# Two depthwise convolutions accumulated in PSUM by VectorE, without tap matmuls, in a three-block transformer kernel

## Chip, cores, metric

One core of one Trainium2 chip runs the whole program. The metric is the device time of one execution in microseconds (us), the median of several.

## The reference, cut to what matters

Three blocks follow one another on x (512 tokens, 1024 channels, float32). The change touches two causal depthwise convolutions: one of 31 taps over 512 channels in the first layer of block 1, and one of 4 taps over 2048 channels in block 3. It also touches the norm of the memory (256 tokens) that cross-attention reads.

```
def _mixer_hgrn2_conv(h, w_in, w_out, lb, out_norm, dw_w, dw_b, ln_g, ln_b):
    proj = h @ w_in
    qz, fz, iz, gz, glu_a, glu_b = split(proj)            # 512 columns each
    f = lb + (1.0 - lb) * sigmoid(fz)
    o = _hgrn2_chunkwise(silu(qz), f, iz)                 # ... gated by silu(gz)
    c = glu_a * sigmoid(glu_b)
    c = _causal_depthwise_conv(c, dw_w, dw_b)             # 31 taps: y_t = sum_k w_k x_{t-30+k} + b
    o_b = silu(_layernorm(c, ln_g, ln_b))
    return concatenate([o_a, o_b]) @ w_out
# mem_n = _rmsnorm(mem, mem_norm); k, v = split(mem_n @ wkv)
# third block: qk = silu(causal_depthwise_conv(concatenate([aq, ak]), conv_w))   # 4 taps
```

## The kernel before, in words

Activations stand as tiles of 128 channels by 512 tokens: `T(i)` is slot i of the SBUF tensor A. Every product with weights is cut into units of 1024x128 weights (`UNITS`). For each unit SP's queue loads RW, ScalarE rounds it to WH (`w_hi`, L261), GpSimd subtracts to get WL (L2709), and TensorE makes 24 matmuls: 8 tiles of input by three passes (L266, L267, L268). WH and WL have three slots, so the weights of unit u + 3 are rounded only after unit u is done. The results go to PSUM banks 0 to 3 in turn; `bank_free` makes unit e wait until VectorE or ScalarE has emptied the bank of unit e - 4. GpSimd does nothing but these subtractions.

The order of work is written by hand. `PLAN` is a list of stages; every engine walks it in order and runs its own part. `Steps.wait_ge` waits for a semaphore; `settle` waits for the engine's own last instruction. `Linear`, `Pairs` and `TokenMajor` are the product stages. With `late=`, the row norm is applied when a unit leaves PSUM (VectorE, L393 or L474), and an activation function follows on ScalarE. In `Linear`, ScalarE applies the function of unit j (which needs VectorE's copy of it) before it rounds the weights of unit j + 3. The hooks `between`, `between_act` and `between_pe` put further work of an engine behind each unit.

In layer 0 the order is: `l0.glu` (8 units, in four pairs, of the gating layer: VectorE scales two banks, ScalarE takes a sigmoid, VectorE multiplies into T(0) to T(3), L496), the memory norm `mem` (class `Late`: on ScalarE `hi` L858 and squares L860, on VectorE `lo` L866 and sums L876 over 8 tiles of 128x256), then `l0.q`, `l0.f`, the memory's `rstd`, `h_gates`, `l0.i`, `h_cum`, `h_query`, `l0.g`, `h_scaled`, `x0.k` (8 units of 256 columns from the memory) and the recurrence (`h_turn`, `h_pe`, `h_vec`).

The 31 taps of the convolution are shared. VectorE does 23 with `depthwise` (L1193, L1199), each tap on all four tiles, from T(k) into T(4 + k), both in SBUF; `conv(st, n)` issues n such rounds: three behind the memory norm and one behind each unit. TensorE does the last eight, as matmuls with diagonal matrices in full float32 (`tap_pe`, L1232), one tile behind each unit of `l0.q`; ScalarE writes those diagonals (`tap_diag`, L1223), and VectorE adds the sums (`tap_add`, L1239). The memory's `rstd` matmuls (L889, L893) wait for the last of these adds because they use banks 6 and 7.

In block 3, `conv3` does the 4 taps behind every second unit of `t.qk` (16 units) with the same `depthwise`, SBUF to SBUF, and `qk_silu` (L2345) follows on ScalarE. Then ScalarE works through `gif_act` (L2354 to L2365), VectorE through `gif_dve`, ScalarE through `stacked_hi`, and `t.v` (TokenMajor, L531 to L533) begins on TensorE as soon as its banks are free. ScalarE rounds the fourth unit of `t.v` behind `stacked_hi`.

Of the kernel before, what the change touches and what calls it, by code (L numbers as in the profile page):

```python
# [27 lines left out]
P = 128  # L28
# [139 lines left out]
def program(nc, io, names):  # L168
    ctx = ExitStack()
    with ctx:  # L170
# [250 lines left out]
        class Pairs:  # L421
# [3 lines left out]
            def __init__(self, name, n, dst, func, of=0, yh=None, acc=False, ready=None, u_off=0, func2=None, late=None, first=1):  # L425
# [8 lines left out]
            def tensor(self, pe, st):  # L434
# [6 lines left out]
                for j in range(first, 2 * self.n):  # L441
                    xh, xl = self.yh if (self.yh is not None and j % 2 == 0) else (XH, XL)
                    pe_tile(pe, st, self.u0 + j, self.e0 + j, xh, xl, S)

            def scalar(self, act, st):
# [5 lines left out]
                for i in range(self.n):  # L451
# [17 lines left out]
                    w_hi(act, st, u + 1 + SPLIT)  # L469

# [5 lines left out]
            def vector(self, dve, st):  # L476
# [4 lines left out]
                for i in range(self.n):  # L481
# [19 lines left out]
                    names[f"ev{e}"] = names[f"ev{e + 1}"]  # L501

# [336 lines left out]
        class Late:  # L839


            def __init__(self, id, gain, ready, left, sq, x, hi, lo, acc, r, rc, b, cols, after, lag):
# [3 lines left out]
                PLAN.append(self)  # L846
# [4 lines left out]
            def scalar(self, act, st):  # L851
                for k in range(KT):
                    if self.after is not None and k < KT - 1:
                        st.wait_ge(*reached(f"{self.after}.free{k}"))
                    if k == 4:
                        w_hi(act, st, self.unit)
                    st.wait_ge(*reached(self.ready(k)))
                    st.do(nc.scalar.activation(self.hi[:, k, 0:self.cols], self.x(k), ACT.Copy, scale=vec(self.gain, k)), f"{self.id}.hi{k}")  # L858
                    if k in self.left:
                        st.do(nc.scalar.activation(self.sq(k), self.x(k), ACT.Square), f"{self.id}.sq{k}")  # L860
# [54 lines left out]
        def late(id, gain, ready, left, sq, x=lambda k: X[:, k, :], hi=None, lo=None, acc=None, r=None, rc=None, b=4, cols=S, after=None,  # L915
                 lag=KT):
            return Late(id, gain, ready, left, sq, x, XH if hi is None else hi, XL if lo is None else lo,
                        SD[:] if acc is None else acc, NR[:, 0, :] if r is None else r, rc, b, cols, after, lag)
# [250 lines left out]
        def lb_ratio(st):  # L1169
# [13 lines left out]
        Pairs("l0.glu", 4, at(0), ACT.Sigmoid, of=1, ready="n0", late=n0)  # L1183
        mark("glu.done", "vector")
        memsq = A[:, 32:36, :].rearrange("p a (b c) -> p (a b) c", c=MEM)
        mem = late("mem", "mem_norm", ready=lambda k: "mem.in", x=lambda k: memt[:, k, :], hi=MH, lo=ML, left=range(KT),
                   sq=lambda i: memsq[:, i, :], acc=T(37)[:, 0:MEM], r=NR[:, 1, 0:MEM], rc=SM[:, 156:158], b=6, cols=MEM)

        def depthwise(st, src, dst, taps, w, b, n, k0=0, first=None, last=0):

            for k in range(n if first is None else 0):
                x, y = src(k), dst(k)
                st.do(v.tensor_scalar(y, x, vec(w, (k0 + k) * taps + taps - 1), vec(b, k) if b else 0.0, ALU.mult, ALU.add))  # L1193
            for t in range(taps - 2 if first is None else first, last - 1, -1):
# [7 lines left out]
        tap = [None]  # L1202

        def conv(st, n):

            for i in range(n):
                if tap[0] is None:
                    depthwise(st, lambda k: T(k), lambda k: T(4 + k), 31, "conv_dw_w", "conv_dw_b", 4, first=None, last=30)
                    tap[0] = 29
                elif tap[0] >= PT:  # L1210
                    depthwise(st, lambda k: T(k), lambda k: T(4 + k), 31, "conv_dw_w", "conv_dw_b", 4, first=tap[0], last=tap[0])
                    tap[0] = tap[0] - 1

        vs(lambda st: conv(st, 3))
        PT = 8

        def tap_diag(st, k):
            for n in range(PT):
                if k >= 2:
                    st.wait_ge(*reached(f"tap.sum{k - 2}"))  # L1220
                elif n == 0:
                    st.wait_ge(consts_in, 16)
                st.do(a_.activation(W2(24 + 2 * (k % 2), 2)[:, n * P:(n + 1) * P], ident, ACT.Copy, scale=vec("conv_dw_w", k * 31 + n)),  # L1223
                      f"tap.diag{k}")

        def tap_pe(st, k):
            if k == 0:
                st.wait_ge(*reached("n0.r"))
            st.wait("glu.done", f"tap.diag{k}")
            for n in range(PT - 1, -1, -1):  # L1230
                sh = 30 - n
                last = mm(PS[:, 4 + k, sh:S], W2(24 + 2 * (k % 2), 2)[:, n * P:(n + 1) * P], T(k)[:, :S - sh], start=(n == PT - 1), stop=(n == 0))  # L1232
            st.do(last, f"tap.sum{k}")

        def tap_add(st, k):
            st.wait_ge(*reached(f"tap.sum{k}"))
            st.settle()
            sh = 31 - PT
            st.do(v.tensor_tensor(T(4 + k)[:, sh:], T(4 + k)[:, sh:], PS[:, 4 + k, sh:S], ALU.add), f"tap.added{k}")  # L1239

        def first_diags(act, st, e):
            tap_diag(st, 0)
            w_hi(act, st, U0["l0.q"] + 1)
            tap_diag(st, 1)
        Stage(scalar=first_diags)

        def q_act(st, j):
            if j < 2:
                tap_diag(st, j + 2)
        Linear("l0.q", dst=at(8), func=ACT.Silu, late=n0, between=lambda st, j: conv(st, 1), between_act=q_act, between_pe=tap_pe)  # L1250
        def f_dve(st, j):
            tap_add(st, j)
            conv(st, 1)
        Linear("l0.f", dst=at(12), func=ACT.Sigmoid, late=n0, between=f_dve)

        def mem_pe(pe, st, e):
            st.wait_ge(*reached("tap.added3"))
            mem.rstd_pe(pe, st)
        Stage(tensor=mem_pe, scalar=lambda act, st, e: mem.rstd_act(act, st), vector=lambda dve, st, e: mem.rstd_dve(dve, st))
# [12 lines left out]
        Linear("l0.i", dst=at(16), late=n0, between=lambda st, j: conv(st, 1))  # L1272
# [29 lines left out]
        Linear("l0.g", dst=at(20), func=ACT.Silu, late=n0, between=lambda st, j: conv(st, 1))  # L1302
# [10 lines left out]
        Linear("x0.k", dst=lambda j: keys(0, j), xh=MH, xl=ML, cols=MEM, late=mem)  # L1313
        vs(lambda st: conv(st, 2))
# [96 lines left out]
        vs(lambda st: conv(st, 31))  # L1411
        mark("conv.done", "vector")

        def xv_pe(st, h, m):
            if (h, m) == (0, 0):
                ho.sums(st)
            elif (h, m) == (0, 3):
                ho.spread(st, range(3))
                st.wait("conv.done")
# [29 lines left out]
        TokenMajor("x0.v", 2, lambda h, t: T(2 * t + h), MH, ML, tiles=2, late=mem, pre=["conv.done"], between_pe=xv_pe, between_act=xv_act)  # L1449
# [886 lines left out]
        def conv3(st, j):  # L2336
            if j % 2:
                k = j - 1
                st.settle()
                depthwise(st, lambda q: T(k + q), lambda q: T(16 + k + q), 4, "conv_w3", None, 2, k)  # L2340
                names[f"conv3.{k}"] = (vector_steps, st.n)

        def qk_silu(st, k):
            st.wait_ge(*reached(f"conv3.{k}"))
            st.do(a_.activation(W2(16 + k, 2), W2(16 + k, 2), ACT.Silu), "ml.qk")  # L2345
# [58 lines left out]
        TokenMajor("t.v", 2, lambda h, t: T(2 * t + h), late=tn, pre=["conv3.14"])  # L2404
# [6 lines left out]
        def ml_cols_pe(pe, st, e):  # L2411
            drained(st, e)
            st.wait("ml.rows", "ml.qk")
# [439 lines left out]
```

## Time and profile before

| | us |
|---|---|
| median of 3 runs | 3822.16 (3817.68 to 3828.68) |
| span of the profiled execution | 3821.3 |
| TensorE matmul busy | 3532.8, 92% |
| VectorE busy | 1334.0, 35% |
| ScalarE busy | 1223.7, 32% |
| GpSimd busy | 1292.4, 34% |

The span runs from the first to the last instruction of one execution; that execution's own device time is not shown apart from it. Busy times are sums of instruction durations. Names: PE is TensorE, DVE VectorE, ACT ScalarE, POOL GpSimd. Times in the timeline count from the start of the span.

### The profile page before, as it was taken

To read this page: it belongs to the slowest core of one execution; us is meant where nothing else is said; L and a number is where in the kernel's file an instruction comes from. 1 tells how busy PE (TensorE), PEld (TensorE's weight loads), DVE (VectorE), ACT (ScalarE), POOL (GpSimd) and SP (SyncE) were. 2 spreads that over 40 slices of the span, in tenths; PEclk is the share of its full clock that TensorE was granted. 3 is DMA by queue.
4 is the path that set the end of the run, shared out by engine and by line. 5 is a ranking of instruction groups with operands and counts; after the bars stand their busy time and mean duration, and the time that the engine had idled before them with its cause. 6 is when DMAs were issued, how large, how long until landed. Compare 5 with 4: busy or idle time off the path is not lost. (4 is left out here: it accounts for less than half of the span.)

```text
span 3821.3 us, 39529 instructions
## 1 busy us (share of the span) xinstructions
PE 3532.8 (92%) x16712; PEld 2836.7 (74%) x16712; DVE 1334.0 (35%) x1921; ACT 1223.7 (32%) x1827; POOL 1292.4 (34%) x531
## 2 busy tenths in 40 slices
PE   7999999999999999998987988999998999899987
PEld 5677788877677788875766776888776768777866
DVE  5773421232333312123373444001283251032432
ACT  4333422232443322333332223222234422242232
POOL 3343244433252444421421002444333314314442
PEclk9999999999999999989988998999999999999998
DMA  4122122222131222221221012222222212202231
GB/s 141 55 95 87 56 94 99 94 91 83 39 117 60 94 97 97 94 75 41 89 88 51 1 64 88 93 95 99 77 99 72 77 39 94 88 28 88 89 105 61
DMA packets 82809, 305.34 MB, mean 80 GB/s; under 512 B 8997, under 2 KB 10825, under 8 KB 81354
## 3 DMA queue, kind: packets, MB, share of 16 engines
q1 hardware_dynamic: 78368, 280.61, 21.9%
q10 hardware_dynamic: 4266, 22.21, 1.5%
q8 instruction: 132, 2.16, 0.2%
q14 instruction: 43, 0.35, 0.0%
HBM read 291.77 MB, written 11.02 MB: 79 GB/s over the span
## 5 line engine op out<-in xcount | busy, mean ns | idle before, releaser
L2709 POOL TENSOR_TENSOR WL<-RW,WH 128x1024 fp32r<-128x1024 f32 x527 | 1292.2, 2454 | 2496.4 <-ACT WH L261 2496.4
L266 PE MATMUL PS<-XH,WH 128*128 128x512 f32 x2968 | 1178.5, 397 | 87.1 <-POOL WL L2709 28.6
L267 PE MATMUL PS<-XL,WH 128*128 128x512 f32 x2968 | 1165.7, 393 | 0.0
L268 PE MATMUL PS<-XH,WL 128*128 128x512 f32 x2968 | 1164.7, 392 | 0.0
L261 ACT ACTIVATE WH<-RW 128x1024 fp32r<-128x1024 f32 x527 | 552.9, 1052 | 787.7 <-PE PS L268 662.0
L266 PEld LDWEIGHTS PS<-XH,WH 128*128 128x128 f32 x2968 | 563.7, 190 | 229.6 <-issue 51.5
L267 PEld LDWEIGHTS PS<-XL,WH 128*128 128x128 f32 x2968 | 564.4, 190 | 118.1 <-issue 3.2
L268 PEld LDWEIGHTS PS<-XH,WL 128*128 128x128 f32 x2968 | 563.6, 190 | 119.0
L266 PE MATMUL PS<-YH,WH 128*128 128x512 f32 (+1 forms) x928 | 351.7, 379 | 30.3 <-DVE YL L837 9.7
L267 PE MATMUL PS<-YL,WH 128*128 128x512 f32 (+1 forms) x928 | 350.1, 377 | 0.0
L268 PE MATMUL PS<-YH,WL 128*128 128x512 f32 (+1 forms) x928 | 349.8, 377 | 0.0
L474 DVE TENSOR_TENSOR SG<-PS,NR 128x512 f32<-128x512 f32 x136 | 93.6, 691 | 686.4 <-PE PS L268 686.0
L266 PEld LDWEIGHTS PS<-YH,WH 128*128 128x128 f32 x928 | 176.6, 190 | 65.8 <-issue 14.2
L268 PEld LDWEIGHTS PS<-YH,WL 128*128 128x128 f32 x928 | 176.6, 190 | 31.8
L267 PEld LDWEIGHTS PS<-YL,WH 128*128 128x128 f32 x928 | 176.9, 191 | 31.3
L462 ACT ACTIVATE SG<-SG 128x512 f32<-128x512 f32 x80 | 50.6, 632 | 367.9 <-DVE SG L474 367.9
L1199 DVE SCALAR_TENSOR_TENSOR A<-A,VEC 128x510 f32<-128x510 f32 (+21 forms) x136 | 150.7, 1162 | 1.7
L600 DVE TENSOR_TENSOR YL<-A,YH 128x512 fp32r<-128x512 f32 x66 | 50.3, 773 | 262.6 <-ACT YH L596 262.6
L393 DVE TENSOR_TENSOR A<-PS,NR 128x512 f32<-128x512 f32 (+1 forms) x84 | 52.5, 637 | 204.7 <-PE PS L268 204.4
L596 ACT ACTIVATE YH<-A 128x512 fp32r<-128x512 f32 x66 | 40.7, 629 | 211.4 <-PE PS L268 211.4
L531 PE MATMUL PS<-WH,XH 128*128 128x512 f32 x192 | 79.0, 411 | 20.1 <-DVE A L393 8.6
L496 DVE TENSOR_TENSOR A<-SG,PS 128x512 f32<-128x512 f32 x30 | 20.6, 688 | 216.1 <-PE PS L268 210.5
(464 smaller groups left out, 3355.0 us busy)
## 6 DMA issues: line engine op xcount, KB each, us to landing
RW<-in_units SPq DMA_DIRECT2D x527, 512.0 KB, 3.3
spill<-X ACTq DMA_DIRECT2D x2, 2048.0 KB, 6.9
X<-spill ACTq DMA_DIRECT2D x2, 2048.0 KB, 9.0
X<-in_xT SPq DMA_DIRECT2D x8, 256.0 KB, 6.8
A<-spill ACTq DMA_DIRECT2D x1, 2048.0 KB, 10.4
out_T<-X ACTq DMA_DIRECT2D x1, 2048.0 KB, 7.4
spill<-X ACTq DMA_DIRECT2D x1, 1536.0 KB, 5.1
spill_gates<-X ACTq DMA_DIRECT2D x1, 1536.0 KB, 7.8
```

The costliest lines, as they stand in the source:

```text
L261: nc.scalar.activation(WH[:, u % SPLIT, :], RW[:, u % RAW, :], ACT.Copy).then_inc(split_hi, 1)
L266: mm(out, hi, xh, start=first, stop=False)
L267: mm(out, hi, xl, start=False, stop=False)
L268: return mm(out, lo, xh, start=False, stop=last)
L393: ins = nc.vector.tensor_tensor(self.dst(j), bank(e % 4, self.cols), self.late.r, ALU.mult)
L462: st.do(nc.scalar.activation(SG[:, j, :], SG[:, j, :], self.func), f"pair{e}")
L474: st.do(nc.vector.tensor_tensor(dst, bank((e + q) % 4), self.late.r, ALU.mult), name)
L531: mm(o, xh, wh, start=(k == 0), stop=False)
L596: st.do(nc.scalar.activation(YH[:, self.hslot(k), :], T(k), ACT.Copy), f"{self.name}.hi{k}")
L600: st.do(nc.vector.tensor_tensor(YL[:, self.hslot(k), :], T(k), YH[:, self.hslot(k), :].bitcast(F32), ALU.subtract), f"{self.name}.lo{k}")
L1199: st.do(v.scalar_tensor_tensor(out=y[:, sh:], in0=x[:, :S - sh], scalar=vec(w, (k0 + k) * taps + t), in1=y[:, sh:], op0=ALU.mult, op1=ALU. ...
L2709: nc.gpsimd.tensor_tensor(WL[:, u % SPLIT, :], RW[:, u % RAW, :], WH[:, u % SPLIT, :].bitcast(F32), ALU.subtract).then_inc(split_done, 1)
```

## The change

- VectorE does all 31 taps. Each tap of tile k reads T(k) from SBUF and adds into PSUM bank 4 + k in place. The tiles go one after another, with a `settle` ahead of each tap. Diagonals, tap matmuls and tap adds are gone. ScalarE copies each finished tile with its bias to T(4 + k) (`conv_out`).
- `conv(st, n)` now issues n single taps: 31 between the pairs of `l0.glu`, then 6 behind each unit of `l0.q` and `l0.f`, 5 behind `l0.i`, 4 behind `l0.g`, 1 behind `x0.k`, and the last one after it: 124 in all. The tail of the convolution behind `h_vec` is gone.
- The memory norm runs between the pairs of `l0.glu`: its tiles behind pairs 0 and 1, its `rstd` matmuls behind unit 5, the reciprocals behind pair 3.
- The recurrence's first step, and `x0.v`, wait for `conv.out3`.
- `conv3` sums in banks 4 to 7; `qk_silu` reads PSUM. `t.v` waits for `conv3.6` in place of `conv3.14`.

```diff
-        vs(lambda st: conv(st, 3))
-        PT = 8
-        def tap_diag(st, k):
...
-        def tap_pe(st, k):
...
-        def tap_add(st, k):
...
         def conv(st, n):
...
+            for _ in range(n):
+                if sum(taps_done) == 4 * 31:
+                    return
+                k = sum(taps_done) // 31
+                sh = taps_done[k]
+                w, y = vec("conv_dw_w", k * 31 + 30 - sh), bank(4 + k)
+                st.settle()
+                if sh == 0:
+                    st.do(v.tensor_scalar(y, T(k), w, None, ALU.mult))
+                else:
+                    st.do(v.scalar_tensor_tensor(out=y[:, sh:], in0=T(k)[:, :S - sh], scalar=w, in1=y[:, sh:], op0=ALU.mult, op1=ALU.add),
+                          f"conv.sum{k}")
+                taps_done[k] = sh + 1
+
+        def conv_out(st, k):
+            st.wait(f"conv.sum{k}")
+            st.do(a_.activation(T(4 + k), bank(4 + k), ACT.Identity, bias=vec("conv_dw_b", k)), f"conv.out{k}")
+
+        def glu_act(st, i):
+            if i < 2:
+                for k in range(4 * i, 4 * i + 4):
+                    mem.tile_act(nc.scalar, st, k)
+            elif i == 2:
+                mem.rstd_act(nc.scalar, st)
+
+        def glu_pe(st, j):
+            if j == 5:
+                mem.rstd_pe(nc.tensor, st)
+
+        def glu_dve(st, i):
+            if i < 2:
+                conv(st, 5)
+                for k in range(4 * i, 4 * i + 4):
+                    mem.lo_dve(nc.vector, st, k)
+                for k in range(4 * i, 4 * i + 4):
+                    mem.sum_dve(nc.vector, st, k)
+                conv(st, 4)
+            elif i == 2:
+                conv(st, 11)
+            else:
+                mem.rstd_dve(nc.vector, st)
+                conv(st, 2)
+        Pairs("l0.glu", 4, at(0), ACT.Sigmoid, of=1, ready="n0", late=n0, between=glu_dve, between_act=glu_act, between_pe=glu_pe)
...
-        Linear("l0.q", dst=at(8), func=ACT.Silu, late=n0, between=lambda st, j: conv(st, 1), between_act=q_act, between_pe=tap_pe)
+        Linear("l0.q", dst=at(8), func=ACT.Silu, late=n0, between=lambda st, j: conv(st, 6), between_act=q_act)
...
-        def mem_pe(pe, st, e):
-            st.wait_ge(*reached("tap.added3"))
-            mem.rstd_pe(pe, st)
...
+        Stage(scalar=lambda act, st, e: conv_out(st, 3))
...
-        vs(lambda st: conv(st, 31))
...
-                depthwise(st, lambda q: T(k + q), lambda q: T(16 + k + q), 4, "conv_w3", None, 2, k)
+                if k >= 4:
+                    st.wait(f"ml.qk{k - 4}")
+                depthwise(st, lambda q: T(k + q), lambda q: bank(6 - k % 4 + q), 4, "conv_w3", 2, k)
```

## Rows read from the trace of the kernel before

**Rows 1.** The page: span, and busy time, share and instructions of TensorE.

```profile
span 3821.3 us, 39529 instructions
PE 3532.8 (92%) x16712; PEld 2836.7 (74%) x16712; DVE 1334.0 (35%) x1921; ACT 1223.7 (32%) x1827; POOL 1292.4 (34%) x531
```

**Rows 2.** Timeline, TensorE, 60 to 230 us: start, us, what, [idle before, releaser].

```profile
72.88 8.42 PE L1232 MATMUL PS<-A 128*128 128x489 f32 x16 [5.18 <-DVE A L876]
...
142.18 1.22 PE L889 MATMUL PS<-A,CST 128*128 128x256 f32 x2 [3.15 <-DVE A L1239]
143.19 0.85 PE L893 MATMUL PS<-CST,A 128*128 128x1 f32 x4
...
190.51 0.80 PE L266 MATMUL PS<-XH,WH 128*128 128x512 f32 x1 [6.38 <-POOL WL L2709]
...
215.31 0.36 PE L266 MATMUL PS<-YH,WH 128*128 128x256 f32 x1 [3.86 <-DVE A L393]
```

**Rows 3.** Timeline, ScalarE and GpSimd, layer 0.

```profile
162.47 1.06 ACT L261 ACTIVATE WH<-RW 128x1024 fp32r<-128x1024 f32 x1 [4.38 <-PE PS L268]
...
188.11 5.10 POOL L2709 TENSOR_TENSOR WL<-RW,WH 128x1024 fp32r<-128x1024 f32 x2 [16.66 <-ACT WH L261]
```

**Rows 4.** Busy time by stretch: PE, PEld, DVE, ACT, POOL, clock, DMA share, GB/s.

```profile
190.50:198.00 7.50, 7.49 (x22) 6.03 (x23) 7.46 (x9) 1.58 (x2) 3.38 (x2) 0.65 0.41 140
```

**Rows 5.** Timeline, VectorE, 30 to 240 us.

```profile
30.59 1.29 DVE L474 TENSOR_TENSOR SG<-PS,NR 128x512 f32<-128x512 f32 x2
...
62.30 1.29 DVE L474 TENSOR_TENSOR SG<-PS,NR 128x512 f32<-128x512 f32 x2 [8.73 <-PE PS L268]
...
65.11 4.66 DVE L866 SCALAR_TENSOR_TENSOR YL<-A,VEC,YH 128x256 fp32r<-128x256 f32 x7 [0.66 <-ACT YH L858]
...
70.51 3.25 DVE L876 TENSOR_TENSOR A<-A 128x256 f32<-128x256 f32 x7
...
87.53 4.82 DVE L1199 SCALAR_TENSOR_TENSOR A<-A,VEC 128x508 f32<-128x508 f32 x4
...
148.82 1.92 DVE L1263 TENSOR_SCALAR A<-A,SM 128x512 f32<-128x512 f32 x4
150.77 1.23 DVE L1265 TENSOR_SCALAR A<-A 128x2048 f32<-128x2048 f32 x1
...
173.96 4.57 DVE L1280 TENSOR_TENSOR_SCAN A<-A 128x512 f32<-128x512 f32 x4
...
182.08 2.28 DVE L1300 TENSOR_TENSOR A<-A 128x2048 f32<-128x2048 f32 x1
...
205.95 4.37 DVE L1306 TENSOR_TENSOR SG<-SG,A 128x2048 f32<-128x2048 f32 x1
...
228.57 0.42 DVE L393 TENSOR_TENSOR A<-PS,NR 128x256 f32<-128x256 f32 x1 [2.45 <-PE PS L268]
...
237.98 2.26 DVE L1388 SCALAR_TENSOR_TENSOR SG<-SG,SM,PS 128x128 f32<-128x128 f32 x6
```

**Rows 6.** Single lines of the kernel, whole span: duration in ns min/median/max, first and last start.

```profile
L1199 DVE SCALAR_TENSOR_TENSOR A<-A,VEC x136: 719/742/2976, 75.7 to 2886.1; 128x511 f32<-128x511 f32 x20, 128x510 f32<-128x510 f32 x20, 128x509 f32<-128x509 f32 x20, 128x508 f32<-128x508 f32 x4
...
L474 DVE TENSOR_TENSOR SG<-PS,NR x136: 676/692/693, 30.6 to 3748.7; 128x512 f32<-128x512 f32 x136
...
L1465 DVE SCALAR_TENSOR_TENSOR A<-A,VEC,PS x4: 733/733/733, 298.9 to 300.9; 128x512 f32<-128x512 f32 x4
```

**Rows 7.** Timeline, block 3: TensorE, VectorE, ScalarE around the end of `t.qk`.

```profile
2881.85 0.77 PE L531 MATMUL PS<-WH,XH 128*128 128x512 f32 x1 [7.56 <-DVE A L393]
2905.37 0.79 PE L531 MATMUL PS<-WH,XH 128*128 128x512 f32 x1 [5.25 <-POOL WL L2709]
...
2880.31 1.28 DVE L393 TENSOR_TENSOR A<-PS,NR 128x512 f32<-128x512 f32 x2
...
2882.55 4.30 DVE L1199 SCALAR_TENSOR_TENSOR A<-A,VEC 128x511 f32<-128x511 f32 x6
...
2881.52 0.72 ACT L2354 ACTIVATE A<-A,VEC 4x512 f32<-4x512 f32 x1
```

More of the change, by code:

```diff
@@ L421, in program, with __init__ @@
         class Pairs:
-            def __init__(self, name, n, dst, func, of=0, yh=None, acc=False, ready=None, u_off=0, func2=None, late=None, first=1):
+            def __init__(self, name, n, dst, func, of=0, yh=None, acc=False, ready=None, u_off=0, func2=None, late=None, first=1,
+                         between=None, between_act=None, between_pe=None):
+                self.between, self.between_act, self.between_pe = between, between_act, between_pe
                 self.name, self.n, self.dst, self.func, self.of, self.acc, self.ready = name, n, dst, func, of, acc, ready
@@ L469, in scalar @@
                     w_hi(act, st, u + 1 + SPLIT)
+                    if self.between_act is not None:
+                        self.between_act(st, i)
             def scaled(self, st, e, q, dst, name):
@@ L501, in vector @@
                     names[f"ev{e}"] = names[f"ev{e + 1}"]
+                    if self.between is not None:
+                        self.between(st, i)
         SG = sb("SG", [P, 4, S])
@@ L1181, in program, with depthwise @@
         vs(lb_ratio)
-        Pairs("l0.glu", 4, at(0), ACT.Sigmoid, of=1, ready="n0", late=n0)
-        mark("glu.done", "vector")
         memsq = A[:, 32:36, :].rearrange("p a (b c) -> p (a b) c", c=MEM)
         mem = late("mem", "mem_norm", ready=lambda k: "mem.in", x=lambda k: memt[:, k, :], hi=MH, lo=ML, left=range(KT),
[L1187 to L1194, printed above, removed]
+                   sq=lambda i: memsq[:, i, :], acc=T(37)[:, 0:MEM], r=NR[:, 1, 0:MEM], rc=SM[:, 156:158], b=6, cols=MEM, planned=False)
+        def depthwise(st, src, dst, taps, w, n, k0):
+            for k in range(n):
+                st.do(v.tensor_scalar(dst(k), src(k), vec(w, (k0 + k) * taps + taps - 1), None, ALU.mult))
+            for t in range(taps - 2, -1, -1):
                 sh = taps - 1 - t
@@ L1200, in depthwise @@
                                                  in1=y[:, sh:], op0=ALU.mult, op1=ALU.add))
-        tap = [None]
+        taps_done = [0] * 4
         def conv(st, n):
[L1206 to L1212, printed above, removed]
@@ L1214, in program @@
-        vs(lambda st: conv(st, 3))
-        PT = 8
-        def tap_diag(st, k):
[L1218 to L1224, printed above, removed]
-        def tap_pe(st, k):
[L1227 to L1233, printed above, removed]
@@ L1271, in program @@
         Stage(scalar=h_ln)
-        Linear("l0.i", dst=at(16), late=n0, between=lambda st, j: conv(st, 1))
+        Linear("l0.i", dst=at(16), late=n0, between=lambda st, j: conv(st, 5))
         SGW = SG[:].rearrange("p a b -> p (a b)")
@@ L1301, in program, with g_act @@
         vs(h_query)
-        Linear("l0.g", dst=at(20), func=ACT.Silu, late=n0, between=lambda st, j: conv(st, 1))
+        def g_act(st, j):
+            if j == 2:
+                conv_out(st, 2)
+        Linear("l0.g", dst=at(20), func=ACT.Silu, late=n0, between=lambda st, j: conv(st, 4), between_act=g_act)
         def h_scaled(dve, st, e):
@@ L1418, in xv_pe @@
                 ho.spread(st, range(3))
-                st.wait("conv.done")
+                st.wait("conv.out3")
                 for k in range(4):
@@ L2412, in ml_cols_pe @@
             drained(st, e)
-            st.wait("ml.rows", "ml.qk")
+            st.wait("ml.rows", "ml.qk14")
             for t in range(TT):
```

57 lines of the change are left out of this document (26 added, 31 removed).

## The prediction

> **What bounds the kernel.** I read the page first: TensorE is busy for 92% of the span [rows 1]. A change pays only if it takes matmuls away or closes a gap in that row, so next I looked for the gaps of TensorE in the timeline. In layer 0 there are five that bear on this change, and each names its cause [rows 2]: 5.18 us ahead of the tap matmuls (VectorE and then ScalarE are still at the memory norm and the first diagonals), 3.15 us ahead of the memory's `rstd` (the last tap add), 6.38 us ahead of the last unit of `l0.g` (its weights are late), 3.86 us in `x0.k` (a bank not emptied, since VectorE is at `h_scaled`), and about 1 us on late weights. The tap matmuls are work of TensorE itself: four tiles of 16 records, 8.4 us for the first [rows 2] and about 28 us in all. A gap also costs afterwards: in the stretch from 190.5 us, behind the 6.38 us gap, the granted clock is 0.65, so TensorE stands at its lower level (1.2 GHz) for part of it [rows 4]. That unit took 8.0 us where a unit at full clock takes 1.06 + 4.38 = 5.44 us [rows 3].
>
> The stretch to measure is from the end of `l0.glu` (62.3 us, where VectorE takes the last pair) to the end of `x0.k` (228.5 us) [rows 5]: 166 us. Needed in it are 16 units of 5.44 us, 8 of 0.42 + 2.45 = 2.87 us [rows 5] and the `rstd` (142.18 to about 144.0, so 1.8 us [rows 2]): 112 us. The other 54 us are taps (28), gaps (19.6) and slow clock (about 7). That is the most that this part can give.
>
> **The price of a tap.** Before, a round of four taps takes 4.82 us, 1.2 us a tap [rows 5], although one lasts 742 ns by the median: the longest lasted 2976 ns [rows 6]. GpSimd's subtraction of about 2.5 us [rows 3] holds up a VectorE instruction with both inputs in SBUF. An instruction with one input in PSUM is not held: 136 scalings of L474, among the same subtractions, lie between 676 and 693 ns [rows 6]. The new taps have that form, but they also write PSUM, and each waits for the one before. No row shows a VectorE write to PSUM. For the chain: six steps of 128 columns, each behind the last, take 2.26 us, 0.38 us each; 512 columns against 256 cost 0.692 - 0.42 us more [rows 5, 6], 1.06 ns a column, so 0.39 us for the 369 more columns of a mean tap (497). I take **0.77 us**. From below, the unblocked six of block 3 go at 4.30 / 6 = 0.72 us [rows 7]; a little less, 0.70, is my lower end. The upper end is the old 1.2 us. I stay by the lower rows: the same operation with SBUF or PSUM as second operand takes 742 and 733 ns [rows 6].
> The Trainium skill, page "VectorE: DVE Perf Modes", section "The TRN2 errata", gives a fixed 120 cycles for a source in PSUM against 58 in SBUF. By that page a tap would be about 65 ns dearer, an estimate of about 0.84 us, and the result about 6 us later than my sum; the two medians just compared speak against it.
>
> **Part 1: the memory norm under `l0.glu`.** This is where the change costs. Pair 0 leaves VectorE at 30.59 + 1.29, plus 0.2 for the sigmoid and 0.7 for the product: 32.7 us [rows 5]. Then come 5 taps (3.85), 4 `lo` and 3 sums at 3.25 / 7 = 0.46 us [rows 5] (3.3), and 4 taps (3.1). `lo` and sums have two SBUF inputs, and ScalarE's rounding for the next unit ends just as they begin, so I add one hit of 2.4 us: 45.4 us. Pair 1 (2.15), 5 taps (3.85), 4 `lo`, 4 sums (3.7) and another hit (2.4): the last sum is ready at 57.5 us. TensorE finishes unit 5 two units before 62.3, at 51.4, and its `rstd` waits there: a new gap of 6.1 us, then the 1.8 us of `rstd` and 2 us of slow clock as behind the 3.15 and 6.38 us gaps. `l0.q` begins 9.9 us late, at 72.2. The tiles that ScalarE now does earlier (8 of 0.7 us) push its weight rounding, but unit 6 is rounded by 48 us and unit 8 by 63 us, before TensorE wants them.
>
> **Part 2: q, f, i.** A unit costs VectorE 0.73 + 6 x 0.77 = 5.35 us, just under 5.44, so TensorE sets the pace, with no taps and no gap. Two diagonal stages and the tap adds vanish from ScalarE and VectorE beside it. Units q0 to g2 take 15 x 5.44: g2 ends at 153.8.
>
> **Part 3: the late weights of g3 stay.** VectorE has f3 at 72.2 + 43.5 = 115.7, its scaling and taps until 121.1, the gates (1.92 + 1.23 [rows 5]) until 124.3, four units of `l0.i` at 0.73 + 5 x 0.77 = 4.58 until 142.6, then `h_cum` and `h_query` (173.96 to 182.08 + 2.28 [rows 5]: 10.4) until 153.0. From there to the weights of g3 the old chain (copy, table load, function, rounding, subtraction) took 190.51 - 184.36 = 6.15: g3 starts at 159.2, behind a gap of 5.4 us, and with the slow clock takes 8.0: 167.2.
>
> **Part 4: `x0.k`.** VectorE takes g3 and 4 taps (until 171.0) and `h_scaled`, 4.37 twice [rows 5] (both inputs SBUF, so still held): 179.8; bank 0 is free at 180.2. TensorE has done k0 to k3 at 167.2 + 11.5 + 1 = 179.7, so the 3.86 us gap shrinks to 0.5. `x0.k` ends at 191.7 in place of 228.5: **-36.8 us**.
>
> **Part 5: behind it.** The last two taps and the copy of tile 3 (1.5 + 0.7 us) now stand ahead of ScalarE's first `h_turned`, which TensorE's third group of transposes waits for: +2.0. The eight old taps that delayed `h_vec` by 0.6 us are gone: **+1.4 us** together. The other old tail taps lay beside `x0.v` and cost nothing. No DMA is added, and SP's loads follow GpSimd's subtractions as before; ScalarE's four copies (0.7 us each) lie under units, and the two further table loads (1.3 us each) under `l0.glu`.
>
> **Part 6: block 3.** TensorE finished `t.qk` at 2881.85 - 7.56 = 2874.3 and waited for VectorE, which emptied the last two banks only at 2881.6 [rows 7]. Now two units cost VectorE 1.3 + 2 x 0.69 + 4.3 = 7.0 us against 10.9, so it is no longer late: `t.v` begins at 2875.1, 6.8 earlier. But its fourth unit needs ScalarE, which reaches `gif_act` (before at 2881.52) once it has rounded one unit and done one function behind 2874.3, at 2876.5, 5.0 earlier. The gap of 5.25 us grows by 1.8, and **-5.0 us** remain.
>
> **Sum.** -36.8 + 1.4 - 5.0 = -40.4 us against the profiled execution: 3821.3 - 40.4 = 3780.9. The median of the runs stands 0.9 us above that span, so I give **3782 us**.
>
> **Rivals.**
> *A, the norm fits.* If neither batch of `lo` and sums meets GpSimd, the last sum is ready at 52.7, the gap is 1.3 us with no fall of the clock: 4.8 + 2 us better, 3775; with taps at 0.70 (-3) and an unheld `h_scaled` (-4), 3768. For it: GpSimd is idle over half of the time here. Against it: ScalarE's order puts the subtractions just there. Chance 0.12.
> *B, dearer taps.* At 0.86 us the units of q and f cost VectorE 5.89 us, 3.6 us more over eight than TensorE needs; with 1.3 in `l0.glu`, 1.8 in `l0.i` and 0.4 in `l0.g`, +7 to 8 us: 3790. At 1.02 (the fixed part of a chained step, 0.38 - 0.13 = 0.25 us, paid twice, once for each side of PSUM) about +26: 3808. For it: writes to PSUM are unseen. Chance 0.22, most of it near the low end.
> *C, the hold stays.* If a tap with one SBUF input is held all the same, 1.2 us a tap, VectorE takes 20 us more in q and f, 6 in `l0.glu`, 9 in `l0.i`, 8 in `l0.g`, and block 3 gains nothing: 3815 to 3830, about no change. Against it: L474. Chance 0.06. That the change does not do what it says is not open here: the 64 tap matmuls are gone from the diff.
> *D, slower: one bank, read and written.* Each tap reads and writes the same bank. If the two cannot overlap, every column costs twice, 0.52 us more: a tap of 1.29 us, and at about 105 us per us of tap price +55: 3837. It turns slower than before from a tap of 0.77 + 40.4 / 105 = 1.15 us. For it: no row has a PSUM input and a PSUM output. Against it: updates in place in SBUF cost nothing extra, and reads of PSUM cost none. Chance 0.07.
> *Forecast* 3774 to 3790: 0.50. Something unforeseen between 3790 and 3810, such as a second late wait in `l0.glu`: 0.03.
>
> **Numbers.** The range 3768 to 3802 holds the forecast, A and most of B; C, D and the far end of B stay out, about 0.2. A measurement of this kernel can tell about 0.3%, 11.5 us. Forecast, A and B (and the unforeseen) lie below 3810.7: faster 0.88. Same is C, 0.05, and slower D with the edge of C, 0.07.
>
> **What would show it.** Right: no L1232; the new tap lines at 0.72 to 0.75 us each without a long tail; TensorE waiting for L876 behind unit 5 of `l0.glu`, about 6 us; a gap of about 5 us ahead of g3; `x0.k` ending near 192; `t.v` starting near 2840 and still waiting for its fourth unit. Wrong: taps above 0.85 us (B, C or D, told apart by whether the minimum or only the maximum has grown), no gap behind unit 5 (A), or waits of TensorE for L393 in `l0.q` and `l0.f`.

## The result and the profile after

The kernel after took 3786.88 us (median of four runs, 3778.93 to 3789.79) and the kernel before 3822.47 us (3817.68 to 3828.68, four runs). The ratio is 0.9900, with an interval of 0.9886 to 0.9914: 38 us less, with 33 to 44 us as its ends, where 40 us were forecast. (The two medians by themselves lie 35.6 us apart; the texts below go by the ratio.) The execution that was profiled took 3778.93 us, 8 us under that median; its span of 3777.0 us is 44.3 us below that of before.

The page of the kernel after, against [rows 1]:

```profile
span 3777.0 us, 39403 instructions
PE 3500.4 (93%) x16648; PEld 2820.3 (75%) x16648; DVE 1305.8 (35%) x1949; ACT 1217.4 (32%) x1800; POOL 1287.7 (34%) x531
```

TensorE has 64 instructions less, the tap matmuls, and 32 us less of busy time. The other 12 us of the span are idle time. The new taps, single lines of the kernel after (duration in ns: min, median, max), against [rows 6]:

```profile
L1225 DVE SCALAR_TENSOR_TENSOR PS<-A,VEC,PS x120: 724/740/755, 33.9 to 192.5; 128x511 f32<-128x511 f32 x4, 128x510 f32<-128x510 f32 x4, 128x509 f32<-128x509 f32 x4, 128x508 f32<-128x508 f32 x4
...
L1208 DVE SCALAR_TENSOR_TENSOR PS<-A,VEC,PS x48: 745/752/755, 2771.1 to 2845.1; 128x511 f32<-128x511 f32 x16, 128x510 f32<-128x510 f32 x16, 128x509 f32<-128x509 f32 x16
...
L878 DVE SCALAR_TENSOR_TENSOR YL<-A,VEC,YH x8: 472/477/2628, 36.9 to 54.5; 128x256 fp32r<-128x256 f32 x8
```

A tap in PSUM has no tail: 168 of them, and the longest takes 755 ns. The `lo` of the memory (L878), with both inputs in SBUF, does have one: 2628 ns against a median of 477. The timeline of VectorE, kernel after, against [rows 5] (start, us, what, [idle before, releaser]):

```profile
30.94 1.29 DVE L480 TENSOR_TENSOR SG<-PS,NR 128x512 f32<-128x512 f32 x2
...
36.94 3.81 DVE L878 SCALAR_TENSOR_TENSOR YL<-A,VEC,YH 128x256 fp32r<-128x256 f32 x4
40.79 1.42 DVE L888 TENSOR_TENSOR A<-A 128x256 f32<-128x256 f32 x3
...
51.21 3.75 DVE L878 SCALAR_TENSOR_TENSOR YL<-A,VEC,YH 128x256 fp32r<-128x256 f32 x4
54.99 1.87 DVE L888 TENSOR_TENSOR A<-A 128x256 f32<-128x256 f32 x4
...
82.70 0.69 DVE L393 TENSOR_TENSOR A<-PS,NR 128x512 f32<-128x512 f32 x1
83.43 4.66 DVE L1225 SCALAR_TENSOR_TENSOR PS<-A,VEC,PS 128x506 f32<-128x506 f32 x6
88.14 0.69 DVE L393 TENSOR_TENSOR A<-PS,NR 128x512 f32<-128x512 f32 x1
...
172.78 4.36 DVE L1321 TENSOR_TENSOR A<-A 128x2048 f32<-128x2048 f32 x1
...
191.24 0.42 DVE L393 TENSOR_TENSOR A<-PS,NR 128x256 f32<-128x256 f32 x1 [1.69 <-PE PS L268]
```

Read three things here. Each batch of four `lo` takes about 1.9 us longer than four of 0.48 us would (3.81 and 3.75 us), so one instruction in each is held. A unit of `l0.q` takes VectorE 0.69 + 4.66 = 5.35 us of work and comes every 88.14 - 82.70 = 5.44 us, the pace of TensorE: the two engines run all but level. And the last unit of `x0.k` reaches VectorE at 191.24 us instead of 228.57 us. The gaps of TensorE that remain in the stretch, from its timeline, against [rows 2]:

```profile
56.92 1.22 PE L901 MATMUL PS<-A,CST 128*128 128x256 f32 x2 [5.23 <-DVE A L888]
...
158.48 0.79 PE L266 MATMUL PS<-XH,WH 128*128 128x512 f32 x1 [5.10 <-POOL WL L2723]
...
179.44 0.39 PE L266 MATMUL PS<-YH,WH 128*128 128x256 f32 x1 [1.25 <-POOL WL L2723]
...
194.59 0.66 PE L1339 MATMUL PS<-CST,A 128*128 128x128 f32 x4 [1.78 <-ACT A L1345]
...
262.25 0.76 PE L266 MATMUL PS<-XH,WH 128*128 128x512 f32 x1 [4.48 <-DVE XL L845]
```

The last of these, a wait for the next norm, stands at 297.35 us in the trace of before, in the same form and with the same 4.48 us. It is a good mark for the end of layer 0's mixing, since nothing near it changed: 262.25 - 297.35 = **-35.1 us**. The line of before:

```profile
297.35 0.47 PE L266 MATMUL PS<-XH,WH 128*128 128x512 f32 x1 [4.48 <-DVE XL L837]
```

The experiments below are read at this mark, and it has a scatter that must be kept in mind. The version with block 3 alone changed has the layer 0 of before, and there the mark stands at 299.80 us, 2.4 us later. Five traces have the layer 0 of the kernel after: the mark stands at 261.8 to 263.4 us, and 230.2 to 231.8 us behind VectorE's first pair of `l0.glu` (30.94 us in the trace above). Differences of 1 to 2 us at the mark are no more than this scatter.

In block 3 the same timeline shows the start of `t.v` and its fourth unit, against [rows 7]:

```profile
2840.36 0.47 PE L539 MATMUL PS<-WH,XH 128*128 128x512 f32 x1 [0.99 <-DVE A L393]
2865.33 0.80 PE L539 MATMUL PS<-WH,XH 128*128 128x512 f32 x1 [8.38 <-POOL WL L2723]
2875.31 0.67 PE L539 MATMUL PS<-WH,XH 128*128 128x512 f32 x1 [2.71 <-ACT A L558]
```

For the size of the step, take a point ahead of everything that changed in block 3, the first matmul of `t.qk`, first in the kernel before and then in the kernel after:

```profile
2773.75 0.77 PE L266 MATMUL PS<-XH,WH 128*128 128x512 f32 x1 [7.76 <-DVE XL L866]
```

```profile
2738.81 0.77 PE L266 MATMUL PS<-XH,WH 128*128 128x512 f32 x1 [7.76 <-DVE XL L878]
```

From it to the first matmul of `t.v` it was 108.10 us and is 101.55: 6.55 us less. From it to GpSimd's last subtraction for `t.v` (2924.23 us before, 2883.84 after) it was 150.48 us and is 145.03, so block 3 gives **5.45 us**. Of the 44.3 us, 35.1 + 5.45 = 40.5 are accounted for; the other 3.8 lie in stages that the change does not touch.

### The profile page after: what moved, and what is told of

It reads as the page before. It is cut to its first block and busy times, and to the rows that moved or that the text cites. A ratio compares the mean times of both kernels' runs of the same rounds, so it can differ in the third digit from the quotient of the medians.

```text
span 3777.0 us, 39403 instructions
## 1 busy us (share of the span) xinstructions
PE 3500.4 (93%) x16648; PEld 2820.3 (75%) x16648; DVE 1305.8 (35%) x1949; ACT 1217.4 (32%) x1800; POOL 1287.7 (34%) x531
## 5 line engine op out<-in xcount | busy, mean ns | idle before, releaser
L1225 DVE SCALAR_TENSOR_TENSOR PS<-A,VEC,PS 128x511 f32<-128x511 f32 (+14 forms) x120 | 88.8, 740 | 4.3
```

The costliest lines, as they stand in the source:

```text
L1225: st.do(v.scalar_tensor_tensor(out=y[:, sh:], in0=T(k)[:, :S - sh], scalar=w, in1=y[:, sh:], op0=ALU.mult, op1=ALU.add), f"conv.sum{k}")
```

## The experiments

Where a time is given as "so many us under before", it is the ratio's distance from 1 times the median of the kernel before measured beside it (3823.22, 3826.48, 3827.24 or 3825.04 us). That median rests on 7 to 23 runs. A changed kernel has 4 to 12, and they spread over 6 to 17 us, which is why differences of a few microseconds are read from the traces.

### The kernel after, twice more

> The changed kernel unaltered, timed beside the kernel before on one chip. Theory (the sum of my steps is right, -40.4 us, and the -35.6 us of the two medians is short of it by the scatter of single runs): 3778 to 3786 us where before is 3822, a difference of 38 to 44 us. Rival (something outside the two changed stages gives about 5 us back in most runs): a difference of 33 to 37 us again.

> The kernel after, unchanged, beside the next one on one chip. It has been 38 and 41 us below the kernel before. If its gain is the layer-0 gain of 35.1 us, about 5 us of block 3 and a scatter of some 4 us, it lies 36 to 44 us below the kernel before of this call.

Measured: 3782.84 us, ratio 0.9892 (0.9879 to 0.9905), 41.3 us under before; and 3788.38 us, ratio 0.9899 (0.9885 to 0.9912), 38.7 us under before. The two traces show the end of layer 0 at -33.9 and -35.1 us. The gain is real and of the size forecast; three measurements of the same kernel lie at 38, 41 and 39 us.

### Block 3 alone

```diff
-                depthwise(st, lambda q: T(k + q), lambda q: T(16 + k + q), 4, "conv_w3", None, 2, k)
+                if k >= 4:
+                    st.wait(f"ml.qk{k - 4}")
+                depthwise(st, lambda q: T(k + q), lambda q: bank(6 - k % 4 + q), 4, "conv_w3", None, 2, k)
...
-            st.do(a_.activation(W2(16 + k, 2), W2(16 + k, 2), ACT.Silu), "ml.qk")
+            st.do(a_.activation(A[:, 16 + k:18 + k, :], PS[:, b:b + 2, :], ACT.Silu), f"ml.qk{k}")
...
-        TokenMajor("t.v", 2, lambda h, t: T(2 * t + h), late=tn, pre=["conv3.14"])
+        TokenMajor("t.v", 2, lambda h, t: T(2 * t + h), late=tn, pre=["conv3.6"])
...
```

> The kernel before with the edit of block 3 alone (four taps summed in PSUM); layer 0 as before. Theory (the gain ends at ScalarE's chain behind t.qk, which starts one VectorE lag earlier): 5 us faster than before, the gap ahead of the fourth unit of t.v grows from 5.25 to 7 to 8.4 us. Rival 1 (the 6.8 us by which t.v starts earlier all stay): 7 us. Rival 2 (hidden anyway): 0 to 1 us.

Measured: 3820.68 us, ratio 0.9992 (0.9984 to 1.0001), 3.1 us under before (6.1 under to 0.4 over), by which neither 5 us nor none can be ruled out. The trace decides: from the first matmul of `t.qk` the start of `t.v` comes 6.5 us sooner and its last subtraction 4.3 us sooner. The waits of TensorE there (us in total, times, longest):

```profile
PE PS L531 <- POOL WL L2712: 8.4, 1, 8.4
...
PE PS L531 <- DVE A L393: 1.0, 1, 1.0
```

The 7.56 us wait for VectorE ahead of `t.v` [rows 7] is now 1.0 us, and the wait for the fourth unit's weights has grown from 5.25 to 8.4 us. Part 6 of the prediction describes this, with 5.0 us for the result. What is missing here against the 5.45 us of the kernel after lies behind the late weights: from there to `t.v`'s second half it is 11.07 us here (2902.96 to 2914.03) and 9.98 us in the kernel after (2865.33 to 2875.31).

### The taps summed in SBUF instead of PSUM

```diff
-                w, y = vec("conv_dw_w", k * 31 + 30 - sh), bank(4 + k)
+                w, y = vec("conv_dw_w", k * 31 + 30 - sh), T(4 + k)
```

with `conv_out` reading the same tile. All else, the order above all, is that of the kernel after.

> The changed kernel with one thing undone in layer 0: the same single taps in the same order, but summed in SBUF tiles T(4) to T(7) and not in PSUM. Theory (an instruction of VectorE with both inputs in SBUF waits for GpSimd's subtraction, one with an input in PSUM does not): taps keep a minimum near 0.74 us, but one tap in six or so lasts 2.5 to 3 us; VectorE has about 15 to 20 such hits of about 2.2 us ahead of h_scaled, and the kernel is 30 to 45 us slower than the changed one, about as slow as before. Rival (the order of the taps, one tile at a time, or the place of the memory norm brings the gain and not PSUM): no more than 5 us slower than the changed kernel.

Measured: 3825.31 us, ratio 1.0002 (0.9993 to 1.0012), 42.5 us above the kernel after measured beside it (3782.84). The whole gain is gone. The mark at the end of layer 0 stands at 301.34 us, 39.1 us later than in the kernel after, while block 3, still summed in PSUM, keeps its 5.2 us. Single line, and the waits of TensorE from 0 to 340 us:

```profile
L1225 DVE SCALAR_TENSOR_TENSOR A<-A,VEC x120: 720/742/2834, 34.2 to 230.9; 128x511 f32<-128x511 f32 x4, 128x510 f32<-128x510 f32 x4, 128x509 f32<-128x509 f32 x4, 128x508 f32<-128x508 f32 x4
```

```profile
PE PS L266 <- POOL WL L2723: 26.5, 8, 10.7
...
PE PS L901 <- DVE A L888: 7.8, 1, 7.8
```

The median of a tap is the same, 742 against 740 ns, and only the maximum differs, 2834 against 755. Taken one by one, 29 of the 120 taps last longer than 0.8 us, 53 us too long in all, and each of the 29 begins while a subtraction of GpSimd is running. In the kernel after, 81 of the 120 overlap a subtraction and none is longer than 755 ns. The waits for weights are 26.5 us where the kernel after has 7.0: ScalarE waits for tiles from VectorE between its roundings, so a held tap delays the weights of a later unit. So neither taking the taps off TensorE nor the new order gains anything by itself. They gain because an operand in PSUM keeps GpSimd's subtractions from holding the tap. What sums in PSUM would give in layer 0 with the old order and the eight tap matmuls left in was not tried.
By the Trainium skill, page "SBUF — State Buffer", section "SBUF: two separate sides", the pair of ports that VectorE and GpSimd share is locked for a whole instruction and taken by a VectorE operation with two SBUF inputs; these two maxima agree, and so does the one held `lo` in each batch.

### The memory's rstd two units later

```diff
-            if j == 5:
+            if j == 7:
                 mem.rstd_pe(nc.tensor, st)
```

> The changed kernel with the memory's rstd matmuls moved from behind unit 5 to behind unit 7 of l0.glu, where their sums are long ready. Theory by my steps (the 5.2 us gap and 2 us of slow clock are on the path): 7 us faster. Rival (VectorE is without a pause from 31 to 152 us except 1.4 us behind unit 7, so VectorE sets when the weights of g3 are asked for): the gap behind unit 5 goes, the gap ahead of g3 grows from 5.1 to about 10 us, and the kernel is 0 to 2 us faster.

Measured: 3785.81 us, ratio 0.9896 (0.9882 to 0.9909), 39.8 us under before, which the times cannot tell from the kernel after. Waits of TensorE from 0 to 250 us, and its timeline:

```profile
PE PS L266 <- POOL WL L2723: 11.1, 6, 5.0
```

```profile
128.25 0.79 PE L266 MATMUL PS<-XH,WH 128*128 128x512 f32 x1 [2.38 <-POOL WL L2723]
...
156.65 0.80 PE L266 MATMUL PS<-XH,WH 128*128 128x512 f32 x1 [4.95 <-POOL WL L2723]
...
260.26 0.47 PE L266 MATMUL PS<-XH,WH 128*128 128x512 f32 x1 [4.47 <-DVE XL L845]
```

The gap of 5.23 us is gone, and in its place 4.1 us more are waited for late weights, spread over three more units. The rival has the size right, 0 to 2 us, but not the place: the gap ahead of g3 stayed at 4.95 us and did not grow to 10. The mark at the end of layer 0 stands at 260.26 us, 2.0 us earlier than after. VectorE's share of that can be followed: it takes the last pair 1.4 us sooner (70.46 instead of 71.82 us) and then does the units of `l0.q` and `l0.f` every 5.29 us instead of every 5.43, so it is 2.5 us ahead at the end of `l0.f` (112.8 instead of 115.3 us) and 1.9 us at the start of `l0.g`. The gap that cost most in the sum was not the bound: VectorE was, and the gap was where it showed.

### The late weights of g3 taken ahead

```diff
         def h_exps(act, st, e):
+            w_hi(act, st, U0["l0.g"] + 3)
```

> The changed kernel, with ScalarE's rounding of the weights of the last unit of l0.g put ahead of the three exponentials (it then waits only for unit g0). By TensorE's own rows the 5.1 us gap and 2.5 us of slow clock go: 7.6 us faster than the changed kernel. Theory (VectorE is the bound of this stretch): VectorE reaches g3 at 163.6 in place of 165.8 us, ends h_scaled 2.2 us earlier, and x0.k waits there for its bank: 2 to 3 us faster only, with a new gap of 4 to 5 us in x0.k.

Measured: 3786.72 us, ratio 0.9896 (0.9881 to 0.9911), 39.8 us under before. The timeline of TensorE:

```profile
163.94 0.58 PE L266 MATMUL PS<-YH,WH 128*128 128x256 f32 x1 [4.17 <-POOL WL L2724]
...
260.26 0.76 PE L266 MATMUL PS<-XH,WH 128*128 128x512 f32 x1 [4.48 <-DVE XL L845]
```

The gap did not close. It moved by one unit, to the first of `x0.k`. The weights of g3 are there in time, but rounding them early also puts GpSimd's subtraction early, on top of VectorE's scans. GpSimd and VectorE in this kernel, and VectorE in the kernel after:

```profile
144.68 2.70 POOL L2724 TENSOR_TENSOR WL<-RW,WH 128x1024 fp32r<-128x1024 f32 x1 [3.04 <-ACT WH L261]
142.86 6.72 DVE L1289 TENSOR_TENSOR_SCAN A<-A 128x512 f32<-128x512 f32 x4
```

```profile
141.91 4.57 DVE L1289 TENSOR_TENSOR_SCAN A<-A 128x512 f32<-128x512 f32 x4
```

The four scans take 6.72 us in place of 4.57. ScalarE's exponentials, `l0.g` on VectorE and the next weights all wait for them, so part of what the early rounding saves is paid there. The four runs below that round these weights early show 6.73 us, and all the others 4.57.

The mark stands at 260.26 us, 2.0 us earlier than after, although this execution was late from the start: its first pair reaches VectorE at 33.06 us and not at 30.94. Counted from there to the end of `x0.k` it is 158.9 us here and 160.1 to 160.9 in the five traces with the layer 0 of after, so 1 to 2 us are gained. The rest of the way to the mark is 68.3 us against 69.9 to 71.0, and there the granted clock differs (0.98 against 0.94 to 0.96), which the edit does not touch.

### 21 taps of tile 3 left for later

```diff
+        TAIL = 21
...
-                if sum(taps_done) == 4 * 31:
+                if sum(taps_done) == 4 * 31 - TAIL:
...
         Stage(scalar=lambda act, st, e: conv_out(st, 3))
+        vs(lambda st: tail(st, 10))
...
         Stage(scalar=ho_squares)
+        vs(lambda st: tail(st, 31))
+        mark("conv.done", "vector")
```

`tail` adds that many of the taps left over to T(7) in SBUF; `l0.i` and `l0.g` take four taps behind each of their first three units and none behind the last, `x0.k` none behind its last; behind pair 2 of `l0.glu` there are none, and behind pair 3 six. The edits of the last two experiments are in it too.

> The changed kernel with VectorE relieved: 21 taps of tile 3 are done in SBUF in VectorE's pauses of the recurrence (10 beside the transposes, 11 behind h_vec), no taps behind pair 2 of l0.glu and behind the last units of l0.i, l0.g and x0.k; and with both edits of the last two kernels (rstd behind unit 7, early weights of g3), each of which gave little alone. Theory (VectorE's own sum of work ahead of h_scaled holds layer 0): x0.k ends near 175 to 177 us in place of 191, and the kernel is 13 to 16 us faster than the changed one, 3766 to 3770 where before is 3823. Rival (TensorE's stretch has other limits, such as ScalarE's order): less than 6 us faster.

> The version with 21 taps of tile 3 left for later (10 ahead of the scan), once more. Its ratio was 0.9864 (0.9844 to 0.9884), while its trace showed layer 0 only 2.7 us further ahead than that of the kernel after, 37.8 against 35.1 us. If the trace is the whole account, it comes back 40 to 45 us below the kernel before (0.9883 to 0.9896). If the gain of the first measurement was its own, it stays at 0.986 to 0.987.

Measured: 3772.83 us, ratio 0.9864 (0.9844 to 0.9884), and the second time 3784.67 us, ratio 0.9895 (0.9881 to 0.9909): 52 and 40 us under before. The first figure did not come back. The traces agree better than the times do: the mark at the end of layer 0 is at -37.8 and -37.0 us against the -35.1 of after. But each of the two edits that it takes over has -37.1 us by itself, so at the mark the 21 taps left for later add nothing that can be told from scatter. Timeline of TensorE in the first of them:

```profile
185.21 0.66 PE L1353 MATMUL PS<-CST,A 128*128 128x128 f32 x4 [0.52 <-DVE A L393]
...
199.53 0.77 PE L1388 MATMUL PS<-A 128*128 128x128 f32 x2 [3.48 <-DVE SG L1416]
...
259.51 0.76 PE L266 MATMUL PS<-XH,WH 128*128 128x512 f32 x1 [4.48 <-DVE XL L845]
```

`x0.k` does end 6.5 us earlier than after (VectorE takes its last unit at 184.72 us, there at 191.24), but not at the 175 to 177 us that were expected, and 3.8 of the 6.5 are given back behind it: ten taps stand on VectorE ahead of the recurrence (9.2 us), TensorE waits 3.48 us for VectorE's first products in it (L1416; the texts here call this the scan), and from 196 to 208 us the granted clock is 0.76 and then 0.67. Why `x0.k` ends no sooner can be read too: VectorE, now relieved, pauses 3.1 us for TensorE ahead of the last unit of `l0.i`; its scans and the product behind them are held by the early subtractions and take 6.73 + 4.33 us in place of 4.57 + 2.29; and TensorE starts `x0.k` only at 157.59 us, from where eight units of 2.88 us cannot end before 180.6.

### Fewer of them ahead of the scan

```diff
-        vs(lambda st: tail(st, 10))
+        vs(lambda st: tail(st, 6))
```

> The version that leaves 21 taps of tile 3 for later, with 6 instead of 10 of them ahead of the scan. In the trace of that version the 10 taps took 9.2 us on VectorE and TensorE then waited 3.5 us for the scan's first product; a drop of the granted clock to 0.67 stood behind that pause. Theory (VectorE's work ahead of the scan is the bound there): four taps fewer take the wait away, the clock drop behind it shrinks, and 2 to 4 us come back ahead of the output projection of layer 0; the four taps behind the scan (3.7 us) cost at most 1.3 us, since VectorE paused 2.4 us there. In all 1 to 3 us below the version with 10 and 3 to 6 us below the kernel after of this call. Rival (the stage from the scan to the output projection is bound by ScalarE and the row products, whose end does not move with the start): the start of the output projection stays where it was, 37.8 us ahead of the kernel before, and the time is within 2 us of the version with 10 taps.

Measured: 3782.31 us, ratio 0.9886 (0.9867 to 0.9905), 43.6 us under before. That is 5 us below the kernel after measured beside it (0.9899), as expected, but the two intervals overlap and the trace shows no such gain. Waits of TensorE from 0 to 340 us, and the two groups of taps in VectorE's timeline:

```profile
PE PS L810 <- DVE SD L805: 5.9, 1, 5.9
...
PE PS L1388 <- DVE SG L1416: 0.6, 1, 0.6
```

```profile
187.29 6.13 DVE L1239 SCALAR_TENSOR_TENSOR A<-A,VEC 128x502 f32<-128x502 f32 x6 [1.40 <-ACT A L1245]
...
209.39 17.49 DVE L1239 SCALAR_TENSOR_TENSOR A<-A,VEC 128x496 f32<-128x496 f32 x15
226.91 3.35 DVE L805 RECIPROCAL SD<-SD 128x512 f32<-128x512 f32 x1
```

The wait for the scan went as the theory had it (3.5 to 0.6 us). Its price was wrong: 15 taps in SBUF took 17.49 us, 1.17 us each, and not the 0.92 of the ten before (one of those ten was held, three of these fifteen), so the reciprocal behind them came late and TensorE waited 5.9 us for it instead of 1.2. The mark is back at 262.27 us, where the kernel after has it (counted from the first pair, which is 1.4 us late here, 230.0 us against 230.2 to 231.8). The three held taps begin at 216.28, 220.62 and 223.40 us, each during one of GpSimd's subtractions for `x0.v`, and they have both inputs in SBUF.

### The late weights of t.v taken ahead

```diff
+            w_hi(act, st, U0["t.v"] + 5)
             st.wait("ml.rows")
```

> The changed kernel with one line in block 3: ScalarE rounds units 3, 4 and 5 of t.v in the 7.6 us in which it waits for VectorE's scans. Theory (the gap of 8.4 us ahead of the fourth unit of t.v is only ScalarE's order; GpSimd then also holds up some of the scans, which nothing on TensorE waits for soon): the gap goes with its slow clock, 8 to 11 us faster than the changed kernel. Rival (the scans held up by GpSimd, or the banks emptied late, put the same wait into the second half of t.v): less than 4 us.

> The kernel after with one weight rounding of t.v taken ahead, once more. Its ratio to the kernel before was 0.9870 (0.9856 to 0.9885), while the unchanged kernel after had 0.9892 and 0.9899; its trace showed no local gain, since the pause of 8.4 us ahead of the fourth unit of t.v only moved to the first unit of the second half (8.2 us). If the trace is the whole account, the ratio comes back at 0.989 to 0.990 (36 to 42 us below the kernel before). If the edit has a gain that the trace of one execution did not show, it stays at 0.986 to 0.988.

Measured: 3778.16 us, ratio 0.9870 (0.9856 to 0.9885), and 3778.35 us, ratio 0.9882 (0.9868 to 0.9897): 50 and 45 us under before. The second expectation rests on a misreading: it held the pause as moved without loss, from absolute times, but that execution came into `t.v` 5 us later than that of after. Measured from the start of `t.v`, there is a gain. TensorE, VectorE and GpSimd in the timeline of the first:

```profile
2845.57 0.47 PE L539 MATMUL PS<-WH,XH 128*128 128x512 f32 x1 [0.98 <-DVE A L393]
...
2875.80 0.77 PE L539 MATMUL PS<-WH,XH 128*128 128x512 f32 x1 [8.19 <-ACT A L558]
...
2859.13 6.58 DVE L2389 TENSOR_TENSOR_SCAN A<-NR,A 4x512 f32<-4x512 f32 x2
2865.74 2.43 DVE L2391 TENSOR_SCALAR A<-A 8x512 f32<-8x512 f32 x1
...
2858.95 8.94 POOL L2724 TENSOR_TENSOR WL<-RW,WH 128x1024 fp32r<-128x1024 f32 x3 [10.72 <-ACT WH L261]
```

From the start of `t.v` to its second half it is 2875.80 - 2845.57 = 30.2 us, and 2873.03 - 2842.80 = 30.2 us in the trace of the second measurement; the kernel after takes 2875.31 - 2840.36 = 34.9 us. That is 4.7 us less, twice, and 3.9 us less at the last subtraction of `t.v`. The hold has a share in the rest: GpSimd's three subtractions in a row now lie on VectorE's scans, which took 2.33 us in the kernel after and take 6.58 us beside them. The rows that ScalarE waits for come late, and TensorE's wait of 8.2 us is for ScalarE. How much more there would be without the hold was not tried.

### Both

The last version with ten taps ahead of the scan, and the line above.

> The edits of the last two kernels together. If both theories hold the gains add: 21 to 27 us faster than the changed kernel, 3755 to 3762 us where before is 3823.

Measured: 3777.89 us, ratio 0.9867 (0.9850 to 0.9883), 51 us under before, where 60 to 70 were expected. The mark of layer 0 is at -37.5 us, and from its start to its end `t.v` gains 4.1 us on after. The gain in `t.v` is there; the one in layer 0 is 2.4 us, no more than either small edit shows alone, and not the 14 us on which the expectation rested. This version and the one with `t.v`'s weights alone are the best of the study, and they cannot be told from each other. Both lie below the kernel after: three ratios of 0.9867 to 0.9882 against its three of 0.9892 to 0.9900, though single intervals touch.

## Why the prediction was right

The forecast was 3782 us. Three measurements of the kernel gave 3786.9, 3782.8 and 3788.4, and the range of 3768 to 3802 holds each of their twelve runs. Step by step:

- **The price of a tap** (0.77 us): 4.66 / 6 = 0.777 us in `l0.q`. The argument, that an operand in PSUM escapes the hold, is shown by the sum in SBUF, which takes the whole gain away. The Trainium skill's table (page "VectorE: DVE Perf Modes", section "The TRN2 errata"), by which a PSUM source costs 62 cycles more, does not agree with these rows: 740 ns in PSUM, 742 in SBUF. (The prediction's estimate of 65 ns from that page would, at rival D's 105 us per us of tap price, have made 6.8 us, not 6.) Rivals B and D fall by the same row, C by its maximum. The sum in SBUF is what C describes, taps that are held all the same, in layer 0: C gave it 3815 to 3830 us, and it took 3825.3.
- **Part 1**: a hit of 2.4 us in each batch of `lo` was forecast, and each has one of about 1.9. The sums were ready at 56.9 us (57.5 forecast), the gap is 5.2 us (6.1), and the last pair of `l0.glu` reaches VectorE 71.82 - 62.30 = 9.5 us later (9.9). Rival A needed neither batch to be hit and falls.
- **Part 2**: 5.35 us a unit on VectorE against 5.44 on TensorE was forecast; it is 0.69 + 4.66 = 5.35 of work at a pace of 5.44, and 5.29 a unit where VectorE is behind (the rstd two units later). TensorE waits for nothing there. What the step did not draw from its own figures is that 0.1 us a unit is next to no slack: from 31 to 152 us VectorE pauses for no more than 1.4 us at once.
- **Part 3**: g3 starts at 158.5 us behind 5.1 us (159.2 and 5.4).
- **Part 4**: the shift at the end of `x0.k` is -37.3 us (-36.8). The gap in it is 0.65 + 1.25 us and for late weights, where one of 0.5 us for VectorE was named; a small error in kind.
- **Part 5**: 37.3 - 35.1 = 2.2 us are given back where 1.4 was forecast. The wait for ScalarE is there, 1.8 us (2.0). Parts 1 to 5 together: -35.1 for -35.4. That it is this close is partly luck, since the mark of the layer 0 of before stands at 297.35 us in one trace and at 299.80 in another.
- **Part 6**: 5.0 us were forecast, as 6.8 for the earlier start of `t.v` less 1.8 for its fourth unit. The start gains 6.55 us, and 6.5 to 6.6 in every trace with block 3 changed. The kernel after keeps 5.45, 5.59 and 5.25 us of it in its three traces, and block 3 alone 4.3. The mechanism is right: VectorE's wait shrinks from 7.56 to 1.0 us, and the fourth unit waits longer, 8.4 us against the 7.05 of the sum.

What the sum did not have is the second bound. It treated the 5.2 us behind unit 5 and the 5.1 us ahead of g3 as two prices that could be saved one by one. With the first gap taken away the time goes to late weights elsewhere, since VectorE is full until 152 us. With the second taken away most of it comes back one unit on, partly because GpSimd's earlier subtraction holds the scans. Each edit moves the mark by 2 us, not by the 7 to 8 that a gap and its slow clock seemed to promise.

## What to carry to other kernels

If VectorE and GpSimd work side by side, the minimum, median and maximum of a line tell what an average hides: a held operation has the same median and a long maximum. An accumulator in PSUM takes the hold away at no price for the step, and here the same order of work takes 1% longer without it. Once an engine runs level with TensorE, a gap on TensorE is a symptom: before pricing its removal, look for the next thing that the same engine owes. When work is moved to an earlier place, ask what GpSimd will then do beside VectorE's operations with two inputs in SBUF. After an experiment measure a stage from its own start, and choose that start behind everything that the edit leaves alone.

## What the hardware showed beyond this

- Writing PSUM from VectorE is not free for every form. `tensor_scalar` on 512 columns takes 0.75 us into PSUM (L1223 of the kernel after, at 33.12 us) and 0.49 us into SBUF (the same line of the version with the sum in SBUF, at 85.24 us). The tap, with its two inputs, costs the same either way.
- One stage that no edit touches takes 3.1 us more in some executions than in others. The norm ahead of `t.qk` has 64 small matmuls in a row, behind 1.6 us of idle time; these are they in the kernel before, the kernel after, and its third measurement:

```profile
2752.46 10.89 PE L703 MATMUL PS<-CST,A 128*128 128x1 f32 x64 [1.63 <-ACT A L742]
```

```profile
2718.02 10.39 PE L711 MATMUL PS<-CST,A 128*128 128x1 f32 x64 [1.62 <-ACT A L750]
```

```profile
2721.78 13.46 PE L711 MATMUL PS<-CST,A 128*128 128x1 f32 x64 [1.63 <-ACT A L750]
```

  The busy time by stretch (PE, PEld, DVE, ACT, POOL, granted clock, DMA share, GB/s), the kernel after and its third measurement:

```profile
2718.00:2721.50 3.50, 3.48 (x31) 3.48 (x32) 3.41 (x6) 3.50 (x7) 0.00 (x0) 1.00 0.00 0
2721.50:2738.00 16.50, 8.98 (x43) 8.60 (x42) 5.62 (x10) 10.08 (x15) 4.65 (x2) 0.51 0.20 64
```

```profile
2722.50:2745.60 23.10, 14.82 (x68) 14.44 (x68) 8.96 (x15) 13.61 (x21) 4.65 (x2) 0.50 0.14 45
```

  In the one, about half of the 64 are done at the full level (clock 1.00, 2.4 GHz) before the clock falls to the lower (0.50, 1.2 GHz), 3.8 us into them. In the other it falls 0.4 us into them. Behind the 64 the two executions run alike: from the first matmul of `t.qk` to that of `t.v` it is 101.55 and 101.53 us. Over all the traces the 64 take 10.4 to 10.9 us (eight traces) or 13.4 to 13.5 (six), whatever the edit. A part of the scatter of 6 to 17 us between runs of one kernel may come from such places; how much of it was not tried.
